# A two-layer decoder step: the attention rebuilt on plain fp32 matmuls, with the work of neighbouring heads laid between row blocks

## What is computed

```python
q = rope((x @ w_q).reshape(bt, l, 8, 2, 64), pos)        # 8 heads, 2 maps of 64
# prompt, in blocks of 128 query rows:
sc = einsum('bqhmd,bkhmd->bhmqk', qi, k) * 64 ** -0.5    # causal mask
p = softmax(sc)
w = p[:, :, 0] - lam * p[:, :, 1]
o = einsum('bhqk,bkhe->bqhe', w, v)                      # v is 128 wide
# each sample: the same over 256 cached keys and values and its own new ones
o = rms_norm(o, subln_g) * (1.0 - lam_init)
y = o.reshape(bt, l, 1024) @ w_o
x = layer_norm(DN_ALPHA * x + y)                         # then the MLP
```

## Time and profile before

| | |
|---|---|
| median of 3 runs | 3813.22 us (3812.39 to 3816.89) |
| profiled execution, own time | 3802.48 us |
| its span, first to last instruction | 3800.7 us |
| mean granted clock of TensorE | 0.926 of 2.4 GHz |
| busy: TensorE, VectorE, ScalarE, GpSimd | 91%, 58%, 26%, 26% |

### The profile page before, as it was taken

How to read it: one execution, slowest core, us unless ns; L and a number is a source line. 1 busy time by engine, 2 the same in 40 slices (tenths; PEclk the granted TensorE clock), 3 DMA queues, 4 the chain that set the end, 5 groups by cost and what they waited for, 6 DMA issues and landing times.

```text
span 3800.7 us, 55918 instructions
## 1 busy us (share of the span) xinstructions
PE 3465.9 (91%) x21178; PEld 3293.7 (87%) x21178; DVE 2221.5 (58%) x3463; ACT 973.7 (26%) x2300; POOL 997.9 (26%) x455
## 2 busy tenths in 40 slices
PE   7999999999996999999988888888886799999997
PEld 7888888888886999999987777777775699999997
DVE  7667767767767633333367666666666753333335
ACT  4333333433332211111113222322232211111112
POOL 3123222222211333433422111111110043333431
PEclk9999999999996999999988888888987799999997
DMA  3111111111110123211102220122110011111111
GB/s 113 36 40 59 48 40 59 42 40 59 42 42 27 45 89 134 89 51 45 45 34 75 62 61 33 44 66 61 61 50 28 12 51 45 45 50 45 45 50 51
DMA packets 85970, 200.85 MB, mean 53 GB/s; under 512 B 8920, under 2 KB 46808, under 8 KB 85248
## 3 DMA queue, kind: packets, MB, share of 16 engines
q1 hardware_dynamic: 35552, 139.54, 10.5%
q10 hardware_dynamic: 50224, 58.37, 4.9%
HBM read 166.93 MB, written 39.60 MB: 54 GB/s over the span
## 4 chain that ended last, share of the span: by engine, by line
issue 65%; PE 19%; POOLq 9%; POOL 5%; SPq 1%; DMA 0%; DVE 0%; ACT 0%; ACTq 0%; DVEq 0%
PE jb L342 19%; POOLq L317 8%; POOL wl L318 5%; SPq L297 1%; DMA wraw<-in_wstream 0%; PE aux L516 0%; ACT acc L937 0%; DVE acc L1346 0%; POOLq L325 0%; POOLq L314 0%; SPq L274 0%; SPq L280 0%; DVE lnq L1350 0%; ACT lnq L925 0%; PE aux L523 0%
## 5 line engine op out<-in xcount | busy, mean ns | idle before, releaser
L315 POOL TENSOR_TENSOR wh<-wraw,one 128x1024 fp32r<-128x1024 f32 x225 | 438.1, 1947 | 2705.7 <-PE jb L342 2253.2
L342 PE MATMUL jb<-xh,wh 128*128 128x344 f32 x2784 | 905.7, 325 | 25.0 <-issue 13.1
L342 PE MATMUL jb<-xl,wh 128*128 128x344 f32 x2784 | 892.4, 321 | 0.0
L342 PE MATMUL jb<-xh,wl 128*128 128x344 f32 x2784 | 892.1, 320 | 0.0
L1162 DVE TENSOR_TENSOR acc<-jb,acc 128x344 f32<-128x344 f32 x672 | 336.3, 515 | 473.2 <-PE jb L342 467.1
L318 POOL TENSOR_TENSOR wl<-wraw,wh 128x1024 fp32r<-128x1024 f32 x225 | 559.6, 2487 | 32.0
L342 PEld LDWEIGHTS jb<-xh,wh 128*128 128x128 f32 x2784 | 526.4, 189 | 33.3 <-issue 20.8
L342 PEld LDWEIGHTS jb<-xl,wh 128*128 128x128 f32 x2784 | 526.0, 189 | 1.7
L342 PEld LDWEIGHTS jb<-xh,wl 128*128 128x128 f32 x2784 | 526.0, 189 | 0.0
L342 PE MATMUL jb<-hh,wh 128*128 128x344 f32 x1536 | 492.2, 320 | 0.0
L342 PE MATMUL jb<-hl,wh 128*128 128x344 f32 x1536 | 490.9, 320 | 0.0
(11 more groups left out here) (251 smaller groups left out, 5658.4 us busy)
## 6 DMA issues: line engine op xcount, KB each, us to landing
wraw<-in_wstream SPq DMA_DIRECT2D x225, 512.0 KB, 3.2
pre<-in_state ACTq DMA_DIRECT2D x16, 512.0 KB, 4.2
out_ssm_s<-pre ACTq DMA_DIRECT2D x16, 512.0 KB, 3.2
kgat<-in_cache_k SPq DMA_DIRECT2D x16, 512.0 KB, 5.4
vgat<-in_cache_v SPq DMA_DIRECT2D x16, 512.0 KB, 6.4
past<-kgat ACTq DMA_DIRECT2D x8, 1024.0 KB, 5.7
past<-vgat ACTq DMA_DIRECT2D x8, 1024.0 KB, 5.9
acc<-in_xT SPq DMA_DIRECT2D x8, 516.0 KB, 7.2
```

Source lines behind the costliest of these rows:

```text
L315: nc.gpsimd.tensor_tensor(wh[slot][:].rearrange("p k m -> p (k m)"), wraw[:, slot].rearrange("p k m -> p (k m)"), one[:].to_broadcast([P, ...
L342: last = mm(jb[:, c, 0:CW], w[slot][:, j * kt + k], x[:, k, cols], start=(k == 0 and p == 0), stop=(k == kt - 1 and p == 2))
```

## The change

All of it lies in the attention; mixer, MLPs, layer norms and the weights' splitting stay. In `before`, `project_head` and `attend` alternate. Now there is one `attend(n)` on each engine, and:

- **Plain fp32.** Scores are one fp32 matmul per map and up to 512 columns, on 64 rows: map 0 on rows 0 to 63 of `qr` and `kr`, map 1 on rows 64 to 127, in turn. Values are one fp32 matmul of 128 columns per key block (`wt` against `vt`), with the query rows as output rows. `q2`, `k2h`, `k2l`, `vth`, `vtl`, the twins and all subtractions for low halves go. The score scale is applied when queries are copied from PSUM.
- **Rotation.** The permutation matmul is replaced by four DMAs that swap blocks of 32 rows (`swap`), for queries and keys.
- **Norm on query rows.** Outputs lie in `os` as 128 queries by 128 features, nine blocks (the ninth holds the samples). The sum of squares is the accumulator of a ScalarE square over a row; the softmax's division by the sum of map 0 is left out and put into the norm (`e9`, `variance`). Then one VectorE multiply, nine transposes (`turn_outputs`), and the cut into `ah` and `al`.
- **Samples.** Scores on VectorE as before, but of head n inside head n; values are 32 matmul passes with padded weights of 8 columns (`wpad`) and 128 moving columns in place of one.
- **Order.** Nine projection chunks (queries, keys and values of head n+1), 24 output chunks of head n-1 and the samples stand between the row blocks of head n. Weight units are read in the order of `HEAD_ORDER`.

The core of the diff:

```diff
-ATT_JOBS, ATT_UNITS = 3 + 8, 3 + 1
-ATT_HEAD_JOBS, ATT_HEAD_UNITS = 5, 5
+ATT_JOBS, ATT_UNITS = 3, 4
-QK_FILL = {2: ((0, 0),), 3: ((0, 1),), 4: ((0, 2),), 5: ((1, 0),), 6: ((1, 1),), 7: ((1, 2),)}
+HEAD_ORDER = (1, 0, 2, 3)
...
-                        for c0 in range(0, width, 512):
-                            w = min(512, width - c0)
-                            out = aux[:, 2 * m_ + c0 // 512, 0:w]
-                            diag = c0 + w == width
-                            for p, kk in enumerate((k2h, k2l)):
-                                last = mm(out, q2[m_][:, rows], kk[m_][:, c0:c0 + w], start=(p == 0),
-                                          stop=(p == 1 and not diag))
+                for c0 in range(0, width, 512):
+                    w = min(512, width - c0)
+                    for m_ in range(2):
+                        mm(aux[:, 2 * m_ + c0 // 512, 0:w], qr[half_of(m_), rows], kr[half_of(m_), c0:c0 + w],
+                           start=True, stop=(c0 // 512 != diag))
...
-                    for k in range(i + 1):
-                        for p, vv in enumerate((vth, vtl)):
-                            last = mm(aux[:, 4, 0:256], vv[:, k], wt[:, k].rearrange("p a b -> p (a b)"),
-                                      start=(k == 0 and p == 0), stop=(k == i and p == 1))
+                for k in range(i + 1):
+                    last = mm(aux[:, 4, 0:128], wt[:, k], vt[:, k], start=(k == 0), stop=(k == i))
...
+            def attend(at, n, fin, ahead):
+                p = n - 1
+                pe.wait_ge(s["rope_done"], 2 * n + 2)
+                scores(n, 0, fin)
+                queries(n, fin)
+                if ahead:
+                    q_slot = unit(at)
+                    fill(q_slot, n, 0, 0)
+                if fin:
+                    values(p, 7, n, 1)
+                turn_values(n)
+                scores(n, 1, fin)
+                turn(n, 0)
+                if ahead:
+                    fill(q_slot, n, 0, 1)
+                pe.wait_ge(s["vt_ready"], n + 1)
+                if fin:
+                    turn_outputs(p)
+                values(n, 0, n, 2)
+                scores(n, 2, fin)
+                turn(n, 1)
+                if ahead:
+                    fill(q_slot, n, 0, 2)
+                if fin:
+                    o_slot = unit(at)
+                    out_jobs(o_slot, p, range(0, 4))
+                values(n, 1, n, 3)
+                scores(n, 3, fin)
+                turn(n, 2)
+                if fin:
+                    out_jobs(o_slot, p, range(4, 8))
+                sample_rows(n)
+                values(n, 2, n, 5)
+                scores(n, 4, fin)
+                turn(n, 3)
...
+            def swap(raw, sw, ready, done, h):
+                act.wait_ge(s[ready], h + 1)
+                for b in range(4):
+                    o_ = b ^ 1
+                    act.dma_start(sw[32 * b:32 * b + 32], raw[32 * o_:32 * o_ + 32]).then_inc(s[done], 16)
...
+            def output(h, i):
+                act.wait_ge(s["o_full"], 8 * h + i + 1)
+                af(os[:, i], aux[:, 4, 0:128], ACT.Copy)
+                last = af(junk[:], aux[:, 4, 0:128], ACT.Square, accum_out=ssq[:, i:i + 1])
...
+            def rope_products(h, raw, sw, swapped):
+                dve.wait_ge(s[swapped], 64 * h + 64)
+                tt(raw[:], raw[:], cos[:], ALU.mult)
+                tt(sw[:], sw[:], sin[:], ALU.mult)
...
+            def combine(n, i):
+                width = (i + 1) * 128
+                dve.wait_ge(s["p_ready"], 16 * n + 2 * i + 2)
+                nc.vector.reciprocal(st[:, 3:4], st[:, 2:3])
+                drain()
+                stt(st[:, 4:5], s1[:, i:i + 1], st[:, 3:4], lam[:, 2:3], ALU.mult, ALU.mult)
+                drain()
+                stt(pp[:, 0:width], pp[:, 1024:1024 + width], st[:, 4:5], pp[:, 0:width], ALU.mult, ALU.add)
...
+            def normalize(p):
+                dve.wait_ge(s["root_done"], p + 1)
+                nc.vector.reciprocal(ro[:, 1], ro[:, 0])
+                drain()
+                tt(os[:], os[:], ro[:, 1].unsqueeze(2).to_broadcast([P, 9, P]), ALU.mult)
```

More of the change, by code:

```diff
@@ new lines, in scores @@
+            def scores(n, i, fin):
+                rows = slice(i * 128, (i + 1) * 128)
+                width = (i + 1) * 128
+                if i:
+                    pe.wait_ge(s["p_ready"], 16 * n + 2 * i)
+                elif fin:
+                    pe.wait_ge(s["p_ready"], 16 * n)
+                if i == 4 and fin:
+                    pe.wait_ge(s["u_free"], 24 * n)
+                diag = (width - 1) // 512
+                for c0 in range(0, width, 512):
[3 more added lines that the diff above has]
+                           start=True, stop=(c0 // 512 != diag))
+                for m_ in range(2):
+                    mm(aux[:, 2 * m_ + diag, width - 128 - 512 * diag:width - 512 * diag], mbf[:, 0], mbf[:, 1],
+                       start=False, stop=True).then_inc(s["s_full"], 1)
@@ new lines, in turn, with m_bank @@
+            def turn(n, i):
+                pe.wait_ge(s["w_ready"], 8 * n + i + 1)
+                for k in range(i + 1):
+                    last = nc.tensor.transpose(jb[:, k // 4, (k % 4) * 128:(k % 4) * 128 + 128],
+                                               pp[:, k * 128:(k + 1) * 128], ident[:])
+                last.then_inc(s["wt_ps"], 1)
+            def m_bank(n, use):
+                count = 11 * n + (use - 2)
+                if not (isinstance(count, int) and count <= 0):
+                    pe.wait_ge(s["m_free"], count)
@@ new lines, in sample_rows @@
+            def sample_rows(n):
+                pe.wait_ge(s["ssc_ready"], n + 1)
+                m_bank(n, 4)
+                mm(aux[0:16, 4, 256:257], qkn[:].rearrange("p m b -> p (m b)"), one[:], start=True, stop=True)
+                for g in range(PAGES):
+                    last = nc.tensor.transpose(aux[0:16, 4, g * 128:(g + 1) * 128],
+                                               ssc[:, g].rearrange("p m b -> p (m b)"), ident[:])
+                last.then_inc(s["srow_full"], 1)
@@ L1473, in project_head, with attend @@
+            def attend(n, fin, ahead):
                 p = n - 1
+                maxima(n, 0)
+                sample_scores(n)
+                combine(n, 0)
                 if fin:
[L1476 to L1485 removed]
```

744 lines of the change are left out of this document (382 added, 362 removed).

## The result

| | before | after |
|---|---|---|
| median of 4 runs each | 3815.05 us (3812.39 to 3821.64) | 3535.47 us (3533.15 to 3538.83) |
| ratio | | 0.9281, 95% interval 0.9258 to 0.9305 |
| profiled execution, own time / span | 3802.48 / 3800.7 us | 3538.83 / 3537.0 us |
| mean granted clock | 0.926 | 0.958 |

The change takes 279.6 us off the medians, a factor of 0.9281. Runs of the kernel before, timed again beside the experiments, lay between 3768 and 3820 us, so ratios of different sets of runs differ by up to 1%; I compare medians of the changed kernels with each other.

The account below looks back on a forecast made before the run. TensorE was taken to bound attention, discounted for idling and a lower clock. Terms 12 + 72 + 530 + 65 + 38 = 717 against 966.9 us, 250 less, gave 3552 profiled and 3563 us as median; range 3490 to 3650.

Parts of the forecast that it names:

- the two discounts: TensorE in attention idles a sixth of the time, and does part of its work at 1.2 instead of 2.4 GHz.
- the discounts stay: Rival: a step counted as covered isn't, clock still falls after idle stretches; 110 us a head, 3710 us; chance 0.13.
- its pair: The mixer stage's busy share 0.92 and clock 0.95, applied to a middle head: 77.2/0.874 = 88.3 us.
- full pace: Rival: no loss but 4 us of waits, clock near 1; 81 to 77 us a head, 3515 to 3487 us; chance 0.08.
- My own walk: Stepping through a middle head's engine queues: 4 us of waits, 77.2 + 4 = 81 us at full clock, a lower bound.
- Six heads: Term for the six middle heads of attention: 530 us.
- the slot count from L470: Score matmuls on alternating row halves, issued in order, take 5 slots for 4 matmuls: 10.8 us a head.
- The price of the half-row form: Changing to half rows and back drains the array, 16 changes a head: at most 2.6 us, left to the range.
- Head 0 and the start: Start, head 0's value projection plus waits: 12 us; head 0 without output, last product and output transposes: 72 us.
- The last head: Head with nothing to project, bound by the chain: 58 us, 65 at a lower clock.
- What follows: Work after the last head: 38 us, where it took 60.2 before.
- What would show it: Expected profile signs: clock near 9, heads of 82 to 96 us, busy above 0.9, two score matmuls 1.3 us, values 0.11.

Follow-up runs that it names:

- table of five kernels: Time a head: before 116.8 us, plain matmuls alone 104.5, changed with projection chunks together 116.0, changed with outputs together 95.5, changed 83.0.
- map by map: Changed kernel with a row block's score matmuls all of map 0, then all of map 1, instead of in turn: 3534.3 us, five of six heads 83.1.
- second profile of the changed kernel: The changed kernel unaltered, run again as yardstick beside the experiments: 3536.72 us, ratio 0.9332.
- the products moved: Changed kernel with VectorE's two query rotation products moved from ahead of block 4's combining to ahead of block 6's and 7's maxima: 3524.00 us, ratio 0.9297.

## Why the prediction was right, and where it was off

**The mechanism held.** I wrote that the work falls only by 5 and the rest must come from the two discounts. The table of five kernels shows it: about the same work, at busy share times clock of 0.95 instead of 0.70. The rival "the discounts stay" was priced at 110 us a head; with the nine chunks out of the blocks a head takes 116.0, so it was the right rival, and chunks between the blocks are what keeps it off. Its reason was not right: the exponential's wait for the transposes, which I held for and against it, is nearly gone without the chunks too (11.3 us in five heads); what comes back are TensorE's waits for copies and sums of ScalarE and VectorE.

**The discount was mis-sized.** "I take its pair: 77.2/0.874 = 88.3": the mixer's pair is not that of these heads. Measured: 83.0, with 0.951 busy and a clock of 1.00, inside the forecast's own 82 to 96 and 2 us above the upper end of "full pace". My own walk gave 4 us of waits a head and 81 at full clock; measured 4.1 of waits and 83.0. The walk was the better estimate and I had used it only as a bound. That its 4 met the 4.1 is in part luck: it had 2 to 4 us in the output chunks, where 1.1 was measured, and nothing at block 4's combining, where 1.7 was. Six heads: 498.2 against 530.

**The work was slightly too low, the scores too high.** From start to start over one middle head: projections 35.1 (priced 33.9), outputs 12.1 (11.3), value products 9.0 (7.9), sample values 3.7 (3.5), scores 9.4 (10.8), the rest 9.7 (9.8); 79.0 against 77.2. The first of a run costs 0.1 to 0.2 us more than the spacing within it, which the prices left out; this and the scores, 1.4 too high, partly cancel. For the scores, the slot count from L470 (8 passes in 0.58 us, 5.3 slots) was the failed step: the price of full overlap, 7.9, was right, with 0.2 us a block behind the last pass. The price of the half-row form, up to 2.6 us a head, stood in the range alone. The Trainium skill (TensorE: Matmul & The Clock Gate, The mechanism) has matmuls on different row groups run side by side, which the 1.92 us against 3.63 bear out. By that section's other statement, matmuls start strictly in program order, map by map should by my count have taken seven slots, an estimated 3.0 us; 1.92 measured and the four 512-column passes in front do not agree with it.

**Head 0 and the start.** 75.1 against 72, and 14.1 against 12; the clock is 0.93 in head 0.

**The last head was too low.** "34 for eight, with 12 for the start and half of VectorE's adds: 58, and 65 at a lower clock": 79.8 to the last value product's start at 2689.5, and 74.8 in the second profile of the changed kernel. The chain was walked without the order of TensorE's queue, where scores stand behind a value product that waits for its weights; swapping the two gave 7 to 10 us back. The rest of the miss is not parted. What follows, 36 against 38.

**The sum.** 2 + 3 - 32 + 13 = -14: 703 against 717. The other 14 us are in the step from profile to median: I set the median 10.7 above the profiled execution, as before, and it lies 3.4 below it. 3563 - 14 - 14 = 3535.

**What would show it.** The clock's row: 8 or 9 in slices 22 to 28, right. A head of 82 to 96, busy above 0.9: 83.0 and 0.95. Two score matmuls of 512 columns in 1.3 us, not 1.7: wrong, 0.43 a pair of passes and so 1.1 (in block 3, 1.06 us). Value passes at 0.11: 14 in 1.58, right. "The exponential's wait for transposes stays": wrong, it went, and not because of the chunks. ScalarE, put at some 44 us a head, is busy for 31.2 (without its DMA issues), and VectorE, put below 75, for 54.6. "Most in the output chunks": 1.1 of 4.1 us only, and the largest wait was the combining behind the rotation products, which I had not walked.

## What to carry to other kernels

Reckon a stage's work at full clock first, then ask what busy share and clock the new order can reach: two kernels with the same work of 80 us took 83 and 116. Independent chunks belong one by one into the places where another engine's chain is under way, and the last iteration, which has none left, wants its own order. Where a walk through the queues gives the waits in microseconds, set it beside the discount of another stage; here it came nearer, though the waits lay elsewhere than it had them.

## What the runs showed of the hardware that I had not expected

**Matmuls on the two halves of the rows start out of program order.** Block 6 of the kernel with the maps apart shows it above. Whether it is so over longer distances than the two matmuls here was not tried, and which part between program and array reorders them is not shown.

**A VectorE pass with two inputs in SBUF takes up to 2.7 times as long beside GpSimd's cuts, a short one far more.** The groups by line and shape, for six heads: the changed kernel, then the one with the products moved (where the lines are L1700 and L1705). Both are the same instructions on the same tiles.

```profile
L1574 DVE TENSOR_TENSOR swq<-swq,sin 128x1032 f32<-128x1032 f32 x6 | 20.3, 3386 | 0.0
L1573 DVE TENSOR_TENSOR rawq<-rawq,cos 128x1032 f32<-128x1032 f32 x6 | 13.3, 2214 | 0.0
```

```profile
L1700 DVE TENSOR_TENSOR rawq<-rawq,cos 128x1032 f32<-128x1032 f32 x6 | 7.4, 1233 | 1.3 <-issue 1.3
L1705 DVE TENSOR_TENSOR swq<-swq,sin 128x1032 f32<-128x1032 f32 x6 | 7.4, 1232 | 0.8
```

What lay beside them, from the timelines of one head of the changed kernel, GpSimd and then VectorE:

```profile
2399.57 1.89 POOL L326 TENSOR_TENSOR wh<-wraw,one 128x1024 fp32r<-128x1024 f32 x1 [14.43 <-PE jb L647]
2401.61 3.17 POOL L329 TENSOR_TENSOR wl<-wraw,wh 128x1024 fp32r<-128x1024 f32 x1
```

```profile
2400.34 2.21 DVE L1573 TENSOR_TENSOR rawq<-rawq,cos 128x1032 f32<-128x1032 f32 x1
2402.48 3.39 DVE L1574 TENSOR_TENSOR swq<-swq,sin 128x1032 f32<-128x1032 f32 x1
```

GpSimd's L329 ends at 2404.78, and the sine product, begun at 2402.48, ends 1.09 us after that, near its undisturbed 1.23: it hardly moved while GpSimd ran. GpSimd's pass is slower too, 3.17 against 2.39 and 2.40 in the same head beside VectorE passes that read one of their two inputs from PSUM, and these (L1605, L1661) keep their usual time. The Trainium skill (GPSIMD Engine Reference, Specifications) says the two engines share their SBUF interfaces and that VectorE instructions with two SBUF inputs contend; the trace agrees. Moving the products took them out of the contention, but not the contention out of the head. They shrink by 3.1 us a head, while VectorE's busy time falls by 0.9 only (322.32 against 327.54 for six heads). Most of the difference is in a small pass of the combining, first in the changed kernel, then with the products moved:

```profile
L1593 DVE SCALAR_TENSOR_TENSOR st<-s,st,lam 128x1 f32<-128x1 f32 x48 | 20.5, 426 | 3.7
```

```profile
L1593 DVE SCALAR_TENSOR_TENSOR st<-s,st,lam 128x1 f32<-128x1 f32 x48 | 33.2, 691 | 3.7
```

It takes some 0.22 us where GpSimd is idle, and 1.87 in block 7 of both kernels; with the products moved it is block 4's that stands beside GpSimd's L329, for 2.33 us. How the 12.7 us divide between the products' new place in the queue and their shorter time no run here shows.
